# Query tiles projected inside layer two's attention, merge gates inside layer six's, heads stored over their own queries, and two early norms reordered

## The reference, cut to what matters

```python
# first block, layer i (0: mla_mixer, 1: swa_mixer)
hn = rmsnorm(x, attn_norm_g[i])
mix, q_cross = swa_mixer(hn, positions, ...)     # proj = hn @ w_in: K, V, 12 query heads, 4 memory heads
cross = memory_cross_attention(q_cross, mem_n, w_mem_kv[i])
x = x + jnp.concatenate([mix, cross], axis=-1) @ w_o[i]
x = x + squared_relu_mlp(rmsnorm(x, mlp_norm_g[i]), mlp_w_up[i], mlp_w_down[i])
# second block
proj = h @ w_in[l]                               # conv inputs, q, k, v, g_nsa, g_merge
y_b = nsa(q, k_cmp, v_cmp, k_sel, v_sel, k_win, v_win, gates)
gm = jax.nn.sigmoid(g_merge)
mix = gm[..., :D_MODEL] * (y_a @ w_a_out[l]) + gm[..., D_MODEL:] * (y_b @ w_b_out[l])
x = x + mix @ w_o[l]
```

## Time and profile before

| what | value |
|---|---|
| time of three runs, median (range) | 1919.3 us (1918.91 to 3840.6) |
| the profiled execution's own time | 1921.03 us |
| its span | 1919.1 us |
| PE matmul busy | 1889.3 us, 98% |
| PE weight load busy | 1575.4 us, 82% |
| DVE, ACT, POOL busy | 872.6, 789.4, 947.3 us (45%, 41%, 49%) |
| mean granted TensorE clock | 0.995 |

### The profile page before, as it was taken

The page is one execution under the profiler, slowest core; times in us unless marked ns, Lnnn a source line. Parts: engine busy times, 40 slices in busy tenths (PEclk is TensorE's granted clock), DMA queues, the critical chain, the costliest instruction groups (busy, mean ns, idle before and its releaser), DMA issues.

```text
span 1919.1 us, 26936 instructions
## 1 busy us (share of the span) xinstructions
PE 1889.3 (98%) x9217; PEld 1575.4 (82%) x9217; DVE 872.6 (45%) x1814; ACT 789.4 (41%) x1412; POOL 947.3 (49%) x1236
## 2 busy tenths in 40 slices
PE   8899999999999999999999999999999999999999
PEld 6778878888888878788888888888888888888887
DVE  6767542222226586432222673697533355444200
ACT  6558643223234477432232353538722342323221
POOL 6650255555556642555555664451055556555553
PEclk9999999999999999999999999999999999999999
DMA  6240123233322311223322222221032223233332
GB/s 212 95 127 2 34 88 99 99 99 93 97 95 94 99 34 46 95 98 99 99 93 98 95 88 88 77 77 35 1 99 94 93 85 112 88 98 98 106 103 77
DMA packets 47437, 168.30 MB, mean 88 GB/s; under 512 B 5616, under 2 KB 5872, under 8 KB 47088
## 3 DMA queue, kind: packets, MB, share of 16 engines
q1 hardware_dynamic: 46368, 164.64, 26.4%
q10 hardware_dynamic: 976, 2.39, 0.4%
HBM read 164.13 MB, written 2.10 MB: 87 GB/s over the span
## 4 chain that ended last, share of the span: by engine, by line
PE 88%; issue 4%; DVE 3%; POOL 3%; ACT 2%; POOLq 0%; ACTq 0%; DVEq 0%
PE bank L580 26%; PE bank L582 26%; PE bank L581 26%; PE bank L697 4%; POOL WL L541 3%; PE bank L664 2%; PE bank L683 2%; DVE XL L1335 1%; ACT PROB L974 1%; PE bank L694 0%; PE bank L824 0%; ACT XH L980 0%; DVE PROB L1413 0%; PE bank L637 0%; PE bank L625 0%
## 5 line engine op out<-in xcount | busy, mean ns | idle before, releaser
L541 POOL TENSOR_TENSOR WL<-RAW,WH 128x256 fp32r<-128x256 f32 x1208 | 929.9, 802 | 927.9 <-ACT WH L910 927.9
L580 PE MATMUL bank<-XH,WH 128*128 128x512 f32 x1439 | 567.0, 394 | 4.0 <-DVE XL L1335 2.6
L582 PE MATMUL bank<-XH,WL 128*128 128x512 f32 x1439 | 560.8, 390 | 0.0
L581 PE MATMUL bank<-XL,WH 128*128 128x512 f32 x1439 | 560.6, 390 | 0.0
L910 ACT ACTIVATE WH<-RAW 128x1024 fp32r<-128x1024 f32 x302 | 316.8, 1052 | 316.2 <-PE bank L582 305.5
L580 PEld LDWEIGHTS bank<-XH,WH 128*128 128x128 f32 x1439 | 270.5, 188 | 63.7 <-DVE XL L1335 5.1
L581 PEld LDWEIGHTS bank<-XL,WH 128*128 128x128 f32 x1439 | 270.7, 188 | 57.1 <-issue 1.9
L582 PEld LDWEIGHTS bank<-XH,WL 128*128 128x128 f32 x1439 | 270.5, 188 | 56.9
L580 PE MATMUL bank<-HH,WH 128*128 128x512 f32 x512 | 199.2, 389 | 0.0
L581 PE MATMUL bank<-HL,WH 128*128 128x512 f32 x512 | 199.2, 389 | 0.0
L582 PE MATMUL bank<-HH,WL 128*128 128x512 f32 x512 | 199.2, 389 | 0.0
(11 more groups left out here) (346 smaller groups left out, 2579.7 us busy)
## 6 DMA issues: line engine op xcount, KB each, us to landing
RAW<-stream SPq DMA_DIRECT2D x302, 512.0 KB, 3.4
out<-X SPq DMA_DIRECT2D x8, 256.0 KB, 4.5
X<-x SPq DMA_DIRECT2D x3, 512.0 KB, 8.3
MEM<-mem SPq DMA_DIRECT2D x1, 1024.0 KB, 10.9
W<-cmp_w ACTq DMA_DIRECT2D x1, 1024.0 KB, 4.6
KT<-KR ACTq DMA_DIRECT2D x1, 768.0 KB, 6.1
CT<-consts SPq DMA_DIRECT2D x1, 513.0 KB, 12.0
X<-x SPq DMA_DIRECT2D x2, 256.0 KB, 3.4
```

The costliest lines, as they stand in the source:

```text
L541: ins = pool.tensor_tensor(WL[:, slot, c], RAW[:, slot, c], WH[:, slot, c].bitcast(F32), ALU.subtract)
L580: pe.matmul(dst, lhs[0], rhs[0], start=start, stop=False)
L581: pe.matmul(dst, lhs[0], rhs[1], start=False, stop=False)
L582: return pe.matmul(dst, lhs[1], rhs[0], start=False, stop=stop)
```

## The change

Four things are changed.

1. **Late queries.** Of the eight query outputs of `in1` two (`EARLY_Q`) stay ahead of `attention("swa")`. The other six are computed inside it, in bank 7 (`LATE_BANK`), one product (three passes) at the start of each of seven steps out of eight, two in the last of these, from step 1 to step 47. DVE drains such an output and writes the remainder of the split, ACT writes the rounded half and converts the weight tiles, and POOL converts between two bias tables. The distances are made on DVE ahead of the last quarter of `mlp0`.
2. **Early gates.** The gates of slabs 0 to 2 (six outputs) are computed inside `attention("nsa")` in bank 7, one product a step, eight steps of ten, and kept in `GATES`. `merge` then takes slab 7 first.
3. **Heads over own queries.** `mla` writes its heads into `MIX0` (over `QT0`) and `swa` into `Q1`/`QX`, so `wo0` and `wo1` have operands of their own, and the new `XH`/`XL` slabs are written output by output.
4. **Early norms.** `scale_columns("mem")` stands ahead of the cosine angles and the sine angles stand behind the squares of `c_kv`; ACT converts one weight tile more at two places of `mem`.

Since bank 7 is taken, `swa` and `nsa` have two transpose banks.

```diff
-        TURNED = {name: [(o + 3) % RING, 4, 7] for name, o in AFTER.items()}
+        TURNED = {name: [(o + 3) % RING, 4, 7][:3 if name == "mla" else 2] for name, o in AFTER.items()}
...
+            early = plan.out_tile[plan.out0["in1"] + 5 + EARLY_Q] + AHEAD + 1
+            lo_parts(converted("wo0"), early)
             pool.wait_ge(signal("dist_done"), 1)
             for h in range(NH):
+                if h >= 2 * EARLY_Q - 2 and h % 2 == 0:
+                    lo_part(early, early % RING)
+                    early += 1
                 bias(h)
...
+            def late_query(tile, k):
+                def step():
+                    t, c, w, _, o, mark, start, stop = in1[late0 + (tile - EARLY_Q) * KD + k]
+                    if start:
+                        pe.wait_ge(drained, o)
+                        pe.wait_ge(lo_done, t + 1)
+                    ins = product(BANK[LATE_BANK][:], (WH[:, t % RING, c:c + w], WL[:, t % RING, c:c + w]),
+                                  (XH[:, k, :], XL[:, k, :]), start, stop)
+                    if mark:
+                        ins.then_inc(products_done, 1)
+                return step
...
+            for tile in range(EARLY_Q, 8):
+                for k in range(KD):
+                    late.setdefault(8 * tile - 15 + min(k, KD - 2), []).append(late_query(tile, k))
+            attention("swa", meanwhile=late)
+            dense(lambda _: plan.steps["wo1"], 0, lambda o, k: over_queries(Q1, k), ready=heads_ready("swa"))
...
+            late = {4: [cmp_turn]}
+            for j in range(2 * EARLY_GATES):
+                for k in range(KD):
+                    late.setdefault(PER_GATE * j + 1 + k, []).append(early_gate(j, k))
+            attention("nsa", meanwhile=late)
...
                 for m in range(KD):
                     keep_ahead(o0 + m)
-                    if m == KD - 1 and not own_operand:
-                        for j in range(KD - 1):
-                            act.wait_ge(signal(stage + "_operand_read"), j + 1)
-                            x_hi(x_stage, norm, j)
                     act.wait_ge(drained, o0 + m + 1)
-                    if own_operand or m == KD - 1:
-                        x_hi(x_stage, norm, m)
+                    x_hi(x_stage, norm, m)
                     square(norm, m, X[:, m, :])
...
-            keep_ahead(memo + 3)
+            keep_ahead(memo + 4)
             std("c_q")
...
-            keep_ahead(memo + 4)
+            keep_ahead(memo + 5)
...
+            late = {8 * tile - 7: late_query(tile) for tile in range(EARLY_Q, 8)}
+            late |= {8 * tile - 14: lambda o=in1 + 6 + tile: keep_ahead(o) for tile in range(EARLY_Q, 8)}
+            attention("swa", late)
...
+            scale_columns("mem", D, NMEM, dst=RMEM)
             dve.wait_ge(signal("pos_in"), 32)
             angles0(0)
-            scale_columns("mem", D, NMEM, dst=RMEM)
-            angles0(1)
             scale_rows("mem", RBM, NMEM)
             for j in range(KKV):
                 add_square("c_kv", j)
             dve.wait_ge(drained, in0 + 5)
             dve.tensor_tensor(KR[HD:QK, :], output(in0 + 5)[HD:QK, :], RBC[HD:QK, :], ALU.mult).then_inc(drained, 1)
+            angles0(1)
             split_value(in0 + 6, 0, PROB1[:, 0, :], RBC, -SCALE)
...
+            for m in range(EARLY_Q + 1):
+                if m < EARLY_Q:
+                    split_value(in1 + 6 + m, s1 + 2 + m, PROB1[:, 2 + m, :], RBC, -SCALE)
+                if m < 3:
+                    dve.wait_ge(drained, in1 + 5 + m)
+                    dve.memset(BANK[SCORES["swa"][m]][:, 2 * P:2 * P + 1], 0.0).then_inc(signal("column_zeroed"), 1)
+                if m:
+                    split_lo_q(s1 + 1 + m, PROB1[:, 1 + m, :], Q1[:, 2 * m - 2:2 * m, :])
...
+            late = {8 * tile - 8: late_query(tile) for tile in range(EARLY_Q, 8)}
+            late |= {8 * tile - 5: late_query_lo(tile) for tile in range(EARLY_Q, 8)}
+            attention("swa", late)
```

More of the change, by code:

```diff
@@ L459, in program @@
         HEAD_OUT = 5, 6
-        AFTER = {"mla": plan.out0["wo0"], "swa": plan.out0["wo1"], "nsa": plan.out0["merge"]}
+        AFTER = {"mla": plan.out0["wo0"], "swa": plan.out0["in1"] + 6 + EARLY_Q, "nsa": plan.out0["gates"]}
         SCORES = {name: [(o + q) % RING for q in range(3)] for name, o in AFTER.items()}
-        TURNED = {name: [(o + 3) % RING, 4, 7] for name, o in AFTER.items()}
+        TURNED = {name: [(o + 3) % RING, 4, 7][:3 if name == "mla" else 2] for name, o in AFTER.items()}
         for units, _, _ in ATTENTION.values():
@@ L1145, in _ @@
             std("in1")
-            for o in range(14):
+            for o in range(6 + EARLY_Q):
                 keep_ahead(in1 + o)
@@ L1432, in attention, with output_projection @@
                                           ).then_inc(signal(name + "_lo"), 1)
-            def output_projection(stage, norm, x_stage, own_operand=False):
+            def output_projection(stage, norm, x_stage):
                 o0 = plan.out0[stage]
                 for m in range(KD + 1):
-                    if m == KD - 1 and not own_operand:
-                        for j in range(KD - 1):
-                            x_lo(x_stage, norm, j)
                     if m < KD:
@@ L1503, in mlp @@
                     chunk(i)
-                if norm_after == "final":
+                if norm_after == "in1":
+                    distances()
+                else:
                     weigh_positions()
@@ L1876, in _ @@
             dve.wait_ge(signal("x_normed"), KD)
[L1877 removed]
+            output_projection("wo2", "norm2", "norm2")
             fo = plan.out0["ffn_up"]
```

255 lines of the change are left out of this document (155 added, 100 removed).

## The result

| | before | changed |
|---|---|---|
| median of the runs (range) | 1920.07 us (1918.91 to 3840.6) | 1907.91 us (1907.46 to 1908.36) |
| the profiled execution, its span | 1921.03, 1919.1 us | 1907.46, 1905.7 us |

The ratio is 0.9932 with the interval 0.9921 to 0.9943: 12 us less, a small gain but clear of none. One run of the kernel before took twice the time of the others (3840.6 us) and stands outside the ratio. Forecast were 1898 us and 21 us less, with a range from 1890 to 1909. The time lies at the edge of that range, so the question is where 9 of the 21 us went.

The account below looks back on a forecast made before the run. PE (matmul) bounds the kernel, busy on 98% of the span, so gains come only from its gaps or slowly spaced passes. Terms -5.1 - 3.8 - 8.5 - 4.0 = -21.4 from 1919.3 us gave 1898, range 1890 to 1909.

Parts of the forecast that it names:

- The term for `swa`: Six outputs moved into swa: 101 us before becomes 92.5, hence -8.5 us (-4 to -12).
- Start (edit 4): Kernel start: PE's waits at two norms, slow passes and a WL wait go, 7.3 us; some returns, net -5.1.
- one weight tile converted sooner covers the 1.37: Start: converting one weight tile sooner on ACT (1.05 us) covers PE's 1.37 us wait for WL at 96.8.
- `wo0`, `wo1` (edit 3): At wo0 and wo1, nearly all PE waiting for the last slabs goes: -3.8 us for both (-3 to -4.2).
- start, wait for the first split: Start of swa: PE waits about 2.3 us for the first query tile's remainder, behind the second's drain on DVE.
- hand-over of bank 7: In swa, PE waits for DVE to drain each late tile: 0.4 us for each of six tiles, 2.4.
- cross units and tail: End of swa: last transposes and copies, which nothing covers, cost 0.9 us.
- the whole difference of 14 us is room: In swa, PE needs 54.2 of the stage's 68.3 us; the 14 us difference can take moved products.
- DVE as the bound, the rival with 0.14: In swa, POOL slows DVE to 14.6 us per tile; swa then loses 4.7, total 1911; chance 0.14.
- `nsa` and `merge` (edit 2): Moved gates fill the hole at nsa's start, 1.4 us, and avoid the clock fall, 2.6: -4.0.
- no fall behind a single gap of 1.7: At nsa's start, with only one 1.7 us gap left ahead, the clock fall costing 2.6 us was expected not to come.
- The banks: Two transpose banks in swa and nsa: priced at 0 and at most 1 us over both stages.

Follow-up runs that it names:

- remainder first: Changed kernel with the remainder of the first query tile split ahead of the second tile's drain on DVE at swa's start: 1906.50 us, 0.9923 of before.
- short split: Changed kernel with the last late query tile's split done on 16 of its 512 columns only: 1905.05 us, 0.9921 of before.
- again: The changed kernel run once more, unaltered, as yardstick and second trace: 1908.17 us, 0.9931 of before.
- spread: Changed kernel with late query tiles spread to one in nine steps instead of eight: 1906.19 us, 0.9922 of before.
- drain sooner: Changed kernel with each late query tile's last products two steps sooner and its drain one step sooner: 1906.50 us, 0.9921 of before.
- both together: Changed kernel with the first query tile's remainder split before the second drain, and late tiles one in nine steps: 1904.18 us, 0.9916 of before.

## Why the prediction was right in its range and the gain 9 us short

That the time lies within 1890 to 1909 is luck in part. The term for `swa` came out at -2.6, outside its own range (-4 to -12), and the whole is inside only since the range was drawn to take in the weak ends of all four terms at once.

**Start (edit 4): -5.1 forecast, -3.8 measured.** The mechanism held. PE reaches the memory diagonal and the sums of `c_kv` without a wait, and no half clock follows in this trace (in two of the other traces with edit 4, those of edits 3 and 4 and of the remainder first, one comes at 81 us). What comes back is more than the 2.2 us I had put. PE in the changed kernel:

```profile
48.43 0.60 PE L666 MATMUL bank<-ACC,CT 128*128 128x256 f32 x2
54.33 0.95 PE L654 MATMUL bank<-CT,ACC 128*128 128x1 f32 x8
79.68 0.36 PE L611 MATMUL bank<-MH_,WH 128*128 128x256 f32 x1 [1.51 <-POOL WL L568]
94.39 0.50 PE L611 MATMUL bank<-XH,WH 128*128 128x512 f32 x1 [1.56 <-DVE VM L1647]
```

The wait for `WL` didn't go, it came 17 us earlier, in `mem`; the conversions of `mem` on DVE are 1.56 us late for the bank of `up0`, and the diagonal of `c_kv` is 0.5 us late. The step that was mis-sized is "one weight tile converted sooner covers the 1.37".

**`wo0`, `wo1` (edit 3): -3.8 forecast, -4.4 measured**, eighteen passes in 4.1 us as forecast.

**`swa` (edit 1): -8.5 forecast, -2.6 measured.** This is the failed step. PE's own work is 86.9 us by the prediction. From the last dense pass to the last value pass it is 98.4 us (644.0 to 742.4) instead of 92.5. The 11.5 us above PE's own work, rounded and summed from the starts in the trace:

| | forecast | measured |
|---|---|---|
| start, wait for the first split | 2.3 | 3.5 |
| half clock from 648.7 to 652.1 | 0 | 1.6 |
| hand-over of bank 7 | 2.4 | 1.9 |
| cross units and tail | 0.9 | 4.3 |
| rest | 0 | 0.2 |

The fourth line is an estimate: from the first cross score to the last value pass PE has 163 pieces (16 units of eight, and 35 that the heads still owe) of 0.91/8 us, 18.6 in all, and takes 22.8 us.

So most of it is the term for the tail, and behind it the sentence that the whole difference of 14 us is room. I took 0.91 us as the time of a cross unit because two of them followed each other so undisturbed. The same trace has the fifteen steps between sixteen cross scores in 14.92 us, 0.99 each, with ACT busy 14.50 of them, and from the first cross score to the last value pass it took 21.1 us, 2.5 above PE's own work. That was there before the change and no late product can fill it, since none stands in those steps; I had left 0.9 for it, 1.6 too little. The other 1.8 (22.8 against 21.1) came with the last tile's split, and the short split takes 1.7 of it back. The two banks have no part in it: the kernel before has 21.1 us there with three and with two. I checked the other engines over the eight steps in which PE has 12.0 us, where they have room, and not over those without a dense product, where ACT has none.

The second part is the half clock. In the kernel before it cost nothing in `swa`, since PE had room; now PE is the bound there, and 3.4 us at half clock cost 1.6. Why it comes at this place stays open. The third is the start, 1.2 us more than forecast, of which 0.9 is the half of a split that ran into POOL's bias table (1.61 instead of 0.69).

**DVE as the bound, the rival with 0.14, is refuted.** DVE is busy 9.12 us in a period of 12.46, not 11.4, and the period is PE's. I had the slowing by POOL in nearly every conversion. It is rarer and smaller beside a conversion, and larger beside a bias table: from 655 to 718 us the scaling of a 256-wide row of `PROB` takes 438 ns in the mean. Of thirteen scalings that overlap a conversion five take 0.50 to 0.56 us and the others 0.35 to 0.37; the three above that (0.77, 0.81 and 1.20) start behind a bias table. All five tables that follow a conversion are in time.

**`nsa` and `merge` (edit 2): -4.0 forecast, or -1.4 if the clock falls; -2.2 measured, and it fell.** The gates fill the two later holes; the wait for all of `in2` stays and is 2.0 us (1.5 before):

```profile
1283.47 0.72 PE L611 MATMUL bank<-XH,WH 128*128 128x512 f32 x1 [2.02 <-DVE VN L1775]
```

The window 1281 to 1292 has a clock of 0.84, where it was 0.69 over as many us. But the kernel without the gates has 0.84 as well, so this is no gain of edit 2 that a run shows. Six kernels with the same code from `in2` on wait 1.7 to 2.0 us there, and have not the same clock. The same window with the remainder first:

```profile
1281.70:1292.70 11.00, 8.98 (x50) 7.49 (x49) 9.24 (x34) 7.07 (x21) 5.80 (x9) 1.00 0.25 79
```

Fifty passes instead of 44. From `nsa`'s first score to the sums of `norm2` it is 265.8, 265.8 and 265.5 us where the clock fell (changed, again, spread) and 264.4, 264.3, 264.1 and 264.1 where it did not (remainder first, drain sooner, short split, both together), so a fall costs 1.5. Its coming doesn't go by the length of the gap: it came behind 2.02, 2.02 and 1.73 us and stayed away behind 2.02, 2.02, 1.76 and 1.76. From before, a trace without the fall is 268.0 - 264.3 = 3.7 shorter, close to 4.0. Against the kernel that lacks edit 2 alone, with a fall in both, it's 1.4 (267.2 and 265.8), which is what the prediction had for that case; the other 0.8 of the 2.2 are there without the gates, and stay open. The premise "no fall behind a single gap of 1.7" was not one that could be had from the trace of one execution. The prediction said from the Trainium skill (TensorE: Matmul & The Clock Gate, What's actually happening) that the moment varies, and gave it no chance of its own; the two executions of one program, one with the clock at 1.00 at 615 us and one with 0.50 at 617, agree with that page.

**The banks: 0 to 1 us forecast.** In `nsa` 0.8 and 1.6 us measured where nothing else stands in the steps, in `swa` nothing that can be told from the half clock, and 0.2 us of waits in `nsa` of the changed kernel.

**Sum.** By the traces -3.8 - 4.4 - 2.6 - 2.2 = -13.0, against -21.4: of the 8.4 us that are missing, 5.9 are `swa`, 1.8 the clock and `nsa`, 1.3 the start, and `wo0` and `wo1` gave 0.6 more.

## What to carry to other kernels

When work moves into a pipeline, check every engine over each kind of step apart, the last ones without the moved work above all: what trails behind the moved work (here a split of 1.25 us on ACT and 1.4 on DVE) lands where those engines have no slack and is paid for the most part. Take a unit's time from the whole run of such units and not from its best pair, and count as room only the steps into which work is really put. Enter a fall of the clock behind a short gap with a chance and its price of 1.5 us, not as a yes or no, and remember that a fall which was free while PE had room costs that price once PE is the bound. An edit's worth below 3 us is read from distances between the same two instructions in traces of kernels that differ in it alone; the median mixes it with falls that come and go elsewhere, as with edit 4, worth 3.8 us in its place and 2.1 in the median.

## What the runs showed of the hardware

**The clock.** A stretch at half clock, 1.2 instead of 2.4 GHz (in the changed kernel 0.50 over all of 648.70 to 652.10), cost 1.5 to 1.7 us wherever PE was the bound (between `mla` and `mlp0`, in `in1`, at the start of `swa` after the change, in `nsa` with the gates). In `swa` of the kernel before (0.50 from 691.6 to 695.0), where PE had room, it cost 0.1 us at most. Whether it comes behind a given short gap differs between executions of one program (at 617 us, behind 1.08 us of idle) and between kernels with the same code there (at `nsa`).

**DVE and POOL.** A half split on DVE that starts just behind one of POOL's bias tables waits for most of it: at the start of `swa` in the changed kernel the half split at 645.02, 0.04 us behind POOL's table of 1.11 us, takes 1.61. It ended at 646.63, 0.54 us behind POOL's end, and its neighbour without such company took 0.69. Where both start together (646.22 and 646.23 with the remainder first), DVE has its 0.70 and POOL takes 1.62 instead of 1.11 (0.01 us is too little to say which came first). So one of the two stands still for the most part of the other's instruction. The Trainium skill (SBUF — State Buffer, SBUF: two separate sides) says that the port they share is locked for a whole instruction when a DVE instruction has two SBUF inputs or runs in its fast form, whichever starts first; the split has two such inputs (`PROB` and `Q`). These rows agree with it, better than the row of 0.72 in the earlier trace rows by which I judged it. But charging every overlap with a whole instruction would be far too much in a sum: of thirteen scaled rows beside a conversion in `swa` five took 0.15 to 0.21 us longer and eight did not, and the mean rose to no more than 438 ns.
